# Delta rule's scan: heads 2 and 3 of each half cross the array, and two PSUM banks take each product

## The reference

```python
def step(state, inp):
    q_c, k_c, u_c, w_c, g_c, attn_c = inp
    v_new = u_c - jnp.einsum('bhcd,bhde->bhce', w_c, state)
    o_c = (jnp.einsum('bhcd,bhde->bhce', q_c * jnp.exp(g_c)[..., None], state)
           + jnp.einsum('bhij,bhje->bhie', attn_c, v_new))
    g_last = g_c[..., -1:]
    state = (state * jnp.exp(g_last)[..., None]
             + jnp.einsum('bhcd,bhce->bhde', k_c * jnp.exp(g_last - g_c)[..., None], v_new))
    return state, o_c
```

## Time and profile before

| what | value |
|---|---|
| median of three runs | 1434.92 us (1433.68 to 1436.06) |
| the profiled execution's own time | 1434.85 us |
| its span, first to last instruction | 1433.0 us |
| mean granted TensorE clock | 0.992 of full speed |
| busy: PE, DVE, ACT, POOL | 1368.5, 890.2, 713.8, 737.5 us |
| scan of half 0, in the span | about 375.7 to 425 us |
| scan of half 1 | about 516.5 to 559 us |

### The profile page before, as it was taken

How to read it: one execution, slowest core, us unless ns; L and a number is a source line. 1 busy time by engine, 2 the same in 40 slices (tenths; PEclk the granted TensorE clock), 3 DMA queues, 4 the chain that set the end, 5 groups by cost and what they waited for, 6 DMA issues and landing times.

```text
span 1433.0 us, 28270 instructions
## 1 busy us (share of the span) xinstructions
PE 1368.5 (95%) x11769; PEld 1237.2 (86%) x11769; DVE 890.2 (62%) x1329; ACT 713.8 (50%) x1150; POOL 737.5 (51%) x821
## 2 busy tenths in 40 slices
PE   6999999999989998999999999899999999999998
PEld 3788887898978887978888998788899999888998
DVE  4788635786977357667454575576634685676533
ACT  2555533764545324455555555655544465555442
POOL 0777653342333223647656574356666444666653
PEclk9999999999999999999999999999999999999999
DMA  9887687543334423557555653435655544456560
GB/s 364 278 272 263 210 305 261 177 163 110 102 117 148 148 96 114 163 196 234 195 178 189 225 177 128 136 119 179 196 194 174 169 147 140 156 176 193 190 200 36
DMA packets 234613, 258.59 MB, mean 180 GB/s; under 512 B 8489, under 2 KB 211703, under 8 KB 234359
## 3 DMA queue, kind: packets, MB, share of 16 engines
q1 hardware_dynamic: 230272, 252.22, 53.7%
q10 hardware_dynamic: 4215, 4.58, 1.0%
HBM read 255.71 MB, written 2.63 MB: 180 GB/s over the span
## 4 chain that ended last, share of the span: by engine, by line
PE 79%; DVE 12%; ACT 4%; issue 2%; DMA 1%; DVEq 0%; SPq 0%; ACTq 0%
PE ps L711 35%; PE ps L705 22%; PE ps L707 11%; DVE w_lo L1940 3%; PE ps L976 2%; DVE arow L1965 1%; ACT w_hi L1334 1%; PE ps L670 1%; PE ps L1020 1%; DVE mt L2194 1%; DMA raw<-in_w_ada 1%; DVE sil L2194 1%; DVE sil L2043 1%; DMA raw<-in_w_ffn_up 1%; PE ps L1043 1%
## 5 line engine op out<-in xcount | busy, mean ns | idle before, releaser
L642 POOL TENSOR_TENSOR w_lo<-raw,w_hi 128x256 fp32r<-128x256 f32 x800 | 722.3, 933 | 678.4 <-ACT w_hi L1334 678.4
L1334 ACT CAST w_hi<-raw 128x1024 fp32r<-128x1024 f32 (+1 forms) x408 | 411.4, 1045 | 178.6 <-PE ps L711 110.6
L705 PE MATMUL ps<-u_hl,w_hi 128*128 128x512 f32 x1216 | 429.9, 398 | 11.4 <-DVE w_lo L1940 5.7
L1940 DVE TENSOR_TENSOR w_lo<-raw,w_hi 128x1024 fp32r<-128x1024 f32 x204 | 276.6, 1356 | 130.4 <-ACT w_hi L1334 128.8
L711 PE MATMUL ps<-u_hl,w_hi 128*128 128x256 f32 x1856 | 350.2, 290 | 7.5 <-DVE yaf L2174 2.7
L707 PE MATMUL ps<-u_hl,w_lo 128*128 128x256 f32 x1216 | 339.9, 280 | 0.0
L711 PEld LDWEIGHTS ps<-u_hl,w_hi 128*128 128x128 f32 x1856 | 291.2, 193 | 19.6 <-issue 9.3
L705 PEld LDWEIGHTS ps<-u_hl,w_hi 128*128 128x128 f32 x1216 | 228.8, 188 | 72.0 <-issue 16.2
L711 PE MATMUL ps<-u_hl,w_lo 128*128 128x256 f32 x928 | 263.8, 284 | 0.0
L707 PEld LDWEIGHTS ps<-u_hl,w_lo 128*128 128x128 f32 x1216 | 229.8, 189 | 0.1
L711 PE MATMUL ps<-mid_hl,w_hi 128*128 128x256 f32 x1024 | 180.8, 280 | 0.0
(11 more groups left out here) (369 smaller groups left out, 1545.4 us busy)
## 6 DMA issues: line engine op xcount, KB each, us to landing
raw<-in_mlp_w SPq DMA_DIRECT2D x64, 1024.0 KB, 5.2
raw<-in_w_ffn_up SPq DMA_DIRECT2D x44, 1024.0 KB, 5.0
raw<-in_w_ada SPq DMA_DIRECT2D x36, 1024.0 KB, 5.7
raw<-in_w_in SPq DMA_DIRECT2D x30, 1024.0 KB, 5.2
raw<-in_w_ffn_down SPq DMA_DIRECT2D x16, 1024.0 KB, 5.3
raw<-in_attn_w_in SPq DMA_DIRECT2D x12, 1024.0 KB, 5.0
raw<-in_mlstm_w_in SPq DMA_DIRECT2D x12, 1024.0 KB, 5.1
raw<-in_w_ffn_down SPq DMA_DIRECT2D x8, 768.0 KB, 4.6
```

Of the source, the lines that this page charges most:

```text
L642: pool.tensor_tensor(w_lo[half][:, kt, :], src[:, kt, :], w_hi[half][:, kt, :].bitcast(F32), ALU.subtract).then_inc(low_ready(n, h)[0], 1)
L705: pe.matmul(two(b - 10 + m), x, z, start=(first and kt == ks.start), stop=False, skip_group_check=True)
L1334: act.copy(w_hi[t % HALVES][:, 0:k, :], src).then_inc(hi_ready, 1)
L1940: dve.tensor_tensor(w_lo[half][:, 0:k, :], src, w_hi[half][:, 0:k, :].bitcast(F32), sub)\
```

## The change

Heads 2 and 3 of each half write their new values crosswise: row half 0 feeds column half 1, and the other way round. The matmuls of lines 1028 and 1043 are issued in the order (head 0, side 0), (head 2, side 0), (head 0, side 1), (head 2, side 1), and so on. Heads 0 and 1 write bank 4, heads 2 and 3 bank 5; the new values take the first 256 columns and the products with `attm` the second 256. So for heads 2 and 3 `ktm`, `attm`, the decay factor of `vns`, `vn` and `vns` live in the opposite partitions, and every reader of these banks is split in two instructions of 256 columns (three where the partitions change: two heads in place, two heads from each side).

```diff
+        def two_heads(b, part):
+            return bank(b)[:, part * S:(part + 1) * S].rearrange("q (h c) -> q h c", h=2)
+        def crossed(h, rows):
+            return SIDES[1 - SIDES.index(rows)] if h >= HG // 2 else rows
+        QUARTERS = [(h, rows) for g in range(HG // 2) for rows in SIDES for h in (g, g + HG // 2)]
 # TensorE
-                    for h in range(HG):
-                        for rows in SIDES:
-                            mm = pe.matmul(bank(4)[rows, h * P:(h + 1) * P], bmat[rows, n, h, :], rr[rows, h, :],
-                                           start=True, stop=True)
+                    for h, rows in QUARTERS:
+                        mm = pe.matmul(bank(4 + h // 2)[crossed(h, rows), h % 2 * P:(h % 2 + 1) * P], bmat[rows, n, h, :], rr[rows, h, :],
+                                       start=True, stop=True)
...
-                                rows = SIDES[side_of(n, d)]
-                                mm = pe.matmul(bank(6 + d)[:, h * P:(h + 1) * P], ktm[rows, p, h, :], vns[rows, h, :],
+                                rows = crossed(h, SIDES[side_of(n, d)])
+                                mm = pe.matmul(bank(6 + (d if h < 2 else 1 - d))[:, h * P:(h + 1) * P], ktm[rows, p, h, :], vns[rows, h, :],
...
-                    for h in range(HG):
-                        for rows in SIDES:
-                            mm = pe.matmul(bank(5)[rows, h * P:(h + 1) * P], attm[rows, n, h, :], vn[rows, h, :],
-                                           start=True, stop=True)
+                    for h, rows in QUARTERS:
+                        x = crossed(h, rows)
+                        mm = pe.matmul(bank(4 + h // 2)[rows, (2 + h % 2) * P:(3 + h % 2) * P], attm[x, n, h, :], vn[x, h, :],
+                                       start=True, stop=True)
 # ScalarE
-                    act.copy(ktm[:, p, :, :], b4(4 + p)).then_inc(s("d_ap"), 1)
+                    act.copy(ktm[:, p, 0:2, :], b4(4 + p)[:, 0:2, :])
+                    for rows in SIDES:
+                        op = act.copy(ktm[crossed(2, rows), p, 2:4, :], b4(4 + p)[rows, 2:4, :])
+                    op.then_inc(s("d_ap"), 1)
...
-                    act.copy(vn, b4(4)).then_inc(s("d_ap"), 1)
+                    for g in range(2):
+                        op = act.copy(vn[:, 2 * g:2 * g + 2], two_heads(4 + g, 0))
+                    op.then_inc(s("d_ap"), 1)
 # VectorE
-                    op = dve.tensor_tensor(attm[:, n], by_pair(7, n), decb[:, n], mul)
+                    dve.tensor_tensor(attm[:, n, 0:2], by_pair(7, n)[:, 0:2], decb[:, n, 0:2], mul)
+                    for rows in SIDES:
+                        op = dve.tensor_tensor(attm[crossed(2, rows), n, 2:4], by_pair(7, n)[rows, 2:4], decb[rows, n, 2:4], mul)
...
-                dve.tensor_tensor(t4(TED), t4(TED), t4(TRK), mul)
+                dve.tensor_tensor(t4(TB)[:, :, 0:2], t4(TED)[:, :, 0:2], t4(TRK)[:, :, 0:2], mul)
+                for rows in SIDES:
+                    dve.tensor_tensor(t4(TB)[crossed(2, rows), :, 2:4], t4(TED)[rows, :, 2:4], t4(TRK)[rows, :, 2:4], mul)
...
-                    b4 = bank(4).rearrange("q (h c) -> q h c", h=HG)
-                    dve.tensor_tensor(vns, b4, wide(t4(TED)[:, n], P), mul).then_inc(s("d_dp"), 1)
+                    for g in range(2):
+                        hs2 = slice(2 * g, 2 * g + 2)
+                        op = dve.tensor_tensor(vns[:, hs2], two_heads(4 + g, 0),
+                                               t4(TB)[:, n, hs2, None].broadcast_to([P, 2, P]), mul)
+                    op.then_inc(s("d_dp"), 1)
...
-                            bd = bank(6 + d).rearrange("q (h c) -> q h c", h=HG)
-                            op = (dve.tensor_tensor(st[:, d], st[:, d], bd, add) if n else dve.tensor_copy(st[:, d], bd))
+                            for g in range(2):
+                                y, x = st[:, d, 2 * g:2 * g + 2], two_heads(6 + (1 - d if g else d), g)
+                                op = dve.tensor_tensor(y, y, x, add) if n else dve.tensor_copy(y, x)
...
-                    b5 = bank(5).rearrange("q (h c) -> q h c", h=HG)
-                    op = dve.tensor_tensor(oacc[:, p], t3, b5, add) if n else dve.tensor_copy(oacc[:, p], b5)
+                    for g in range(2):
+                        hs2 = slice(2 * g, 2 * g + 2)
+                        y, x = oacc[:, p, hs2], two_heads(4 + g, 1)
+                        op = dve.tensor_tensor(y, t3[:, hs2], x, add) if n else dve.tensor_copy(y, x)
```

## The result

The changed kernel takes 1438.71 us (median of 20 runs, 1435.23 to 1442.32), the kernel before 1436.12 in the same sessions (20 runs): a ratio of 1.0019, 95% interval [1.0011, 1.0028]. I had forecast 1434.1 and a range of 1431.2 to 1437.2: the sign was wrong and the range too low. Of the 4.6 us between forecast and median, 1.2 come from the base: I started from 1434.92, the median of three runs of the kernel before, which over 20 runs is 1436.12. The other 3.4 are the change itself, -0.79 forecast and +2.6 measured. The profiled execution took 1438.01, its span is 1436.2.

The account below looks back on a forecast made before the run. The prediction took PE as the bound (79% of the chain, DVE 12%); half 0's +1.64 and half 1's -2.43 summed to -0.79 us, from 1434.92 to 1434.1 us, range 1431.2 to 1437.2.

Parts of the forecast that it names:

- `attm` and the factor: Half 0, DVE before the transposes at 326.86 us: `attm` in 12 instructions +1.07, factor in three +0.16, together +1.23 us.
- slower: Rival, chance 0.11: `attm` products before 326 us cost 0.41 us each instead of 0.195; total +1.7, about 1438 from 0.51 up.
- the group's saving: Lines 1028 and 1043, both scans: each of 16 groups saves 0.40 us of PE, 6.4 us in all.
- half 1's steps: Scan steps 0 to 2 of half 1: each 0.76 us shorter, -2.28 us together.
- half 0's early saving: Steps 0 and 1 of half 0: PE's 1.6 us saved only lengthens the wait before line 1020 to about 3.5 us.
- the clock drop behind it: Half 0, after the wait before line 1020: PE at half clock, +1.5 us (bounds 0 and 1.75).
- no clock drop: Rival, chance 0.24: half 0's wait stays short or PE's activity suffices, so -2.29 us in all, 1432.6 us.
- the readers: Half 0 up to `st`: split `vns` +0.04, `vn` +0.17 and `st` +0.05, together +0.26 us.
- steps 2 and 3 of half 0: Half 0's later scan: four groups save 1.60 us, step 3's `vns`, `vn` and `oacc` add 0.25, together -1.35 us.
- `attm` is hidden in half 1: Half 1's preparation: DVE waits 2.26 us for PE after `attm`, so the +1.23 us costs nothing there.
- more arrives: Rival, chance 0.10: also cheaper 128-element products (0.6 less) and half-clock step 3 of half 1 saving 0.80 a group; -3.3, 1431.5.
- Swallowed: Rival, chance 0.10: the groups' savings do not arrive or quarters don't overlap, split readers' cost remains; +2.1 us, 1437.0 us.

Follow-up runs that it names:

- The part alone, in place: The kernel before with only `attm` split into 12 instructions and the factor of `vns` into three, all written in place: 1437.06 us, ratio 1.0017.

## Why the prediction was wrong

- **The base** was 1.2 too low, as said with the result. It doesn't touch the sign.
- **The step that failed** is the term "`attm` and the factor" of half 0, +1.23, which measured +2.84. The mechanism was right (DVE's work on the way to 326 us is on the chain, all of it arrives); its size was wrong. Of this term's miss of 1.6, `attm` is 1.24 (twelve in 3.64 less 1.33 is +2.31, where I took 1.07) and the factor 0.4 (three instructions and the one behind take 0.75 where 0.20 stood: +0.55, where I took 0.16 and 0.32 at most). I stayed on the line of products that keep their partitions, which is right for those, 0.20 measured. Eleven of these twelve change them. The part alone, in place, shows a loss of the same size (1.0017), and moving it removes the loss (0.9987). The rival *slower* had this place, with 0.41 a product; it is 0.30. With +2.84 in my sum and the 0.26 of the next item it gives +1.1 instead of -0.79: the sign turns. The rest of the +3.2 between the two profiles lies in the terms that follow; of the median's +2.6 that is not shown.
- **The clock behind 326 us.** I left it as it was. With a wait of 5.26 it is at half for longer: 4.90 for transposes and inversion group instead of the 4.64 of the kernel before, another +0.26.
- **Right:** the group's saving, 0.42 to 0.43 for my 0.40; half 1's steps, 0.77 for 0.76; half 0's early saving lost in the wait for `st`, 3.61 us for 3.5; the clock drop behind it, 1.56 for 1.5, so that *no clock drop* did not happen; the readers, +0.33 for +0.26; steps 2 and 3 of half 0, -1.46 for -1.35. `attm` is hidden in half 1: DVE still waits for line 985 behind it, 0.21 us at 467.50 for 2.26 before, and line 720 behind the inversion's second level starts 4.85 us later than before (485.55, 480.70), less than the 5.05 of line 720 at 446 us.
- **Not in the sum:** half clocks in the preparation of half 1, +1.52 at 446 us and, behind the wait of 2.74 us, a longer one than before, +0.75 with what the slab transfer gives back. They differ between executions, and were no rival of mine; I had read the clock from three waits, which it happened to follow in order of their length. From the last head's output to the end another +0.45 stands where I had 0. Between PE's waits before 915.00 and 940.77 us (917.15 and 943.56 after) the shift grows by 0.64, and only the changed kernel is at half clock there, behind its 2.05 us; the rest was not followed up. Against them stands the end of half 1: line 1051 takes 1.13 where 1.97 stood, at half clock in both, which I had put under *more arrives*; the stretch gave -0.87 for -0.36.
- ***Swallowed*** gave about the shift that was measured, +2.1 for +2.6, for a wrong reason: the groups do save their 0.42, and half 1's steps hand it on. The Trainium skill, "TensorEngine Tiling (Array Packing)", section PSUM Bottleneck, says that copies out of PSUM may limit after tiling; half 1's steps don't bear it out (0.77 saved in each). In half 0 PE waits 3.61 us for `st`, which I had called agreement; but the work on the chain ahead of `st` there is mostly convolution and cast, and only its smaller part reads PSUM.
- **Open:** what decides between half and full clock behind waits of 1.5 to 2.7 us; how the median's +2.6 divides between the block and later half clocks; whether `ktm`'s copies cost anything behind 444 us where the clock stays full.

## What to carry to other kernels

When an edit splits one DVE instruction by partitions, read the price from neighbours that change partitions, not from a line through sizes, and group the pieces so that neighbours read and write the same ones. When a part lands on the chain just ahead of a PE wait, look at the clock behind that wait as well, in more than one profile, and see first whether the part can stand behind what PE waits for: here that order alone turned +0.19% into -0.13%. Where a saving ends in a longer wait, cheap extra matmuls in the wait may keep the clock, as they did here. A median of three runs is no base for a forecast to 2 us: here it was 1.2 off.

## What the runs showed of the hardware

- DVE overlaps a product with the one before it only where input and output keep their first partition: 128 columns of fp32 from PSUM start 0.20 to 0.22 us apart then, 0.28 to 0.31 otherwise, whether input, output or both change (between partitions 0 and 64, the only ones tried).
- 64x64 products on four quarters and two banks overlap on PE whether four neighbours in the queue use all four quarters or two of them: 0.44 us for 16 records head after head, 0.42 in the other order, 0.85 with uncrossed places and one bank.
- The same 1.91 us of idle PE was followed by half clock in nine profiles and by full clock in nine; half clock also followed 1.49 us, and full clock 2.68.
- Six fp32 matmul records of 512 columns (2.74 us) in a wait of 3.6 us were followed by full clock, where the same place without them showed 0.50.
